# GDN inverse by levels: 64x64 array quarters replaced by block-diagonal operands in the full array

## The reference, cut to what matters

```python
def _gated_delta_rule(q, k, v, beta, g):
    q, k, v, beta, g = (_chunks(t.astype(F32)) for t in (q, k, v, beta, g))
    gc = jnp.cumsum(g, axis=-1)
    decay = jnp.exp(jnp.where(incl, gc[..., :, None] - gc[..., None, :], -jnp.inf))
    kb = k * beta[..., None]
    lhs = eye + jnp.einsum("nbhik,nbhjk->nbhij", kb, k) * decay * (1.0 - eye)
    solve = functools.partial(lax.linalg.triangular_solve, left_side=True, lower=True, unit_diagonal=True)
    u = solve(lhs, v * beta[..., None])
    w = solve(lhs, kb * jnp.exp(gc)[..., None])
    ...                                   # scan over the chunks with a state
def _gdn_mixer(...):
    qkv = jax.nn.silu(_dwconv(qkv, conv_w))
    q, k = _l2norm(q), _l2norm(k)         # x * rsqrt(sum x^2 + NORM_EPS)
    o = rule(q, k, v, ...) + reversed rule
    o = _rms(o) * norm_w * jax.nn.silu(z)
    return o @ w_out
```

## Time and profile before

| what | value |
|---|---|
| median of 3 runs | 1712.95 us (1711.44, 1712.95, 1870.54) |
| the profiled execution: its own time | 1710.5 us |
| its span, first to last instruction | 1708.7 us |
| mean granted TensorE clock | 0.989 of full speed |
| GDN loop, one turn | 86.7 us |

### The profile page before, as it was taken

One profiled execution on the slowest core, in us unless ns is written; L12 is line 12 of the kernel. 1 busy time (PEld: TensorE's weight loads), 2 busy tenths in 40 slices (PEclk: granted clock), 3 DMA queues, 4 the chain that ended last, 5 costly groups with the idle time before them and its releaser, 6 DMA issues.

```text
span 1708.7 us, 36355 instructions
## 1 busy us (share of the span) xinstructions
PE 1587.3 (93%) x14884; PEld 994.6 (58%) x14884; DVE 902.7 (53%) x1956; ACT 658.1 (39%) x1316; POOL 122.9 (7%) x315
## 2 busy tenths in 40 slices
PE   5999999999999999999999999999999889777798
PEld 2465555656545758676767676777744545343443
DVE  1373552826533758686868686868620642111173
ACT  2152532516213645555555555555510112111123
POOL 7000010000000000000000000000000012122100
PEclk9999999999999999999999999999999979999999
DMA  9340111202102211111111111111054579999941
GB/s 360 98 102 2 49 51 38 62 0 99 57 13 77 78 51 51 51 51 51 51 51 50 51 50 51 51 51 51 2 200 157 229 268 419 421 421 421 399 155 49
DMA packets 105461, 210.93 MB, mean 123 GB/s; under 512 B 10194, under 2 KB 78135, under 8 KB 92028
## 3 DMA queue, kind: packets, MB, share of 16 engines
q1 hardware_dynamic: 99256, 197.52, 31.9%
q0 software_dynamic: 4896, 8.40, 1.3%
q10 hardware_dynamic: 1188, 3.28, 0.5%
HBM read 203.80 MB, written 14.81 MB: 128 GB/s over the span
## 4 chain that ended last, share of the span: by engine, by line
PE 55%; DMA 10%; DVE 4%; ACT 1%; issue 1%; SPq 0%; DVEq 0%; POOL 0%; ACTq 0%; POOLq 0%
PE ps L1497 12%; DMA W<-in_moe_w_up_dram 10%; PE ps L1508 6%; PE ps L2536 5%; PE ps L1669 4%; PE ps L1638 4%; PE ps L3119 3%; PE ps L2933 3%; PE ps L506 2%; PE ps L1538 2%; PE ps L1519 1%; PE ps L1548 1%; PE ps L1560 1%; PE ps L1523 1%; PE ps L2946 1%
## 5 line engine op out<-in xcount | busy, mean ns | idle before, releaser
L1497 PE MATMUL ps<-hT,W 128*128 128x512 f32 x512 | 233.6, 601 | 2.2 <-ACTq L95 2.2
L1497 PEld LDWEIGHTS ps<-hT,W 128*128 128x128 f32 x512 | 96.2, 193 | 101.0 <-issue 99.2
L594 PE MATMUL ps<-hT,W 128*128 128x512 f32 x288 | 143.3, 612 | 0.0
L1508 PE MATMUL ps<-W,hT 128*128 128x256 f32 x512 | 123.7, 387 | 0.0
L2080 DVE SCALAR_TENSOR_TENSOR arena<-ps,arena 128x510 f32<-128x510 f32 (+1 forms) x128 | 95.4, 745 | 14.0 <-ACT arena L1799 10.6
L1508 PEld LDWEIGHTS ps<-W,hT 128*128 128x128 f32 x512 | 92.8, 190 | 12.7
L2536 PE MATMUL ps<-W,yT 128*128 128x512 f32 x216 | 93.1, 592 | 0.9 <-ACT yT L1892 0.9
L1902 ACT ACTIVATE W<-ps 128x512 f32<-128x512 f32 x96 | 57.5, 599 | 74.3 <-PE ps L1638 30.8
L1669 PE MATMUL ps<-W 64*64 64x64 f32 x2304 | 77.1, 220 | 0.0
L1638 PE MATMUL ps<-W,arena 64*64 64x64 f32 x2048 | 68.5, 220 | 6.6 <-DVE spare L189 2.5
L1669 PEld LDWEIGHTS ps<-W 64*64 64x64 f32 x2304 | 72.8, 135 | 2.7 <-issue 2.7
(11 more groups left out here) (543 smaller groups left out, 2896.0 us busy)
## 6 DMA issues: line engine op xcount, KB each, us to landing
W<-in_w_in_dram SPq DMA_DIRECT2D x33, 512.0 KB, 6.7
W<-in_gdn_w_in_dram SPq DMA_DIRECT2D x16, 1024.0 KB, 7.6
arena<-in_moe_w_up_dram SPq DMA_DIRECT2D x16, 1024.0 KB, 25.6
arena<-in_moe_w_down_dram SPq DMA_DIRECT2D x16, 1024.0 KB, 24.2
W<-in_moe_w_up_dram SPq DMA_DIRECT2D x16, 1024.0 KB, 25.3
W<-in_moe_w_down_dram SPq DMA_DIRECT2D x16, 1024.0 KB, 24.4
W<-in_moe_w_gate_dram SPq DMA_DIRECT2D x16, 1024.0 KB, 25.0
arena<-in_moe_w_gate_dram SPq DMA_DIRECT2D x14, 1024.0 KB, 25.5
```

Of the source, the lines that this page charges most:

```text
L594: mm = pe.matmul(ps[:, 5 + i % 2, :], w[:, k, j, :], hT[:, k, :], start=(k == 0), stop=(k == ND - 1))
L1497: mm = pe.matmul(ps[:, 6 + k0 % 2, :], wg[:, k, j * P:(j + 1) * P], hT[:, k, :], start=(k == 0), stop=(k == ND - 1))
L1508: mm = pe.matmul(ps[:, 4 if t < 2 else 1, 256 * (t % 2):256 * (t % 2) + 256], hT[:, k, t * P:(t + 1) * P], wz[:, k, :], start=(k == 0), st ...
```

## The change

For levels 1 to 4 both products use the whole array. `Nn` gets its two off-diagonal quarters cleared by POOL (`clear_corners`), after they were saved to a new tensor `corner` for level 6, so that one 128x128 by 128x64 product does both quarters of V. ACT writes V into a block-diagonal tensor `Vbd` (one copy for each half of the partitions), so that one product with V as the stationary operand does both quarters of T, and gives T itself instead of its transpose. DVE puts the new blocks into `Tgc` and transposes to `TTgc`; step `T g lv` now stands after the transpose. The two groups' V products come first, then z steps, then the two groups' T products; the z steps are dealt out anew, and `k_tokens` and `v_tokens` change places. The epsilons move into the bias of ACT's Ln, the norm weight into the scale of the copy to `yT`, so `norm_eps`, `z_weighted` and half of `o_mean` go. `first_level` of group 0 moves ahead of `output 3`, and the last convolution is split around level 1.

```diff
-    Vgc = half2[:, 4096:5120].rearrange("p (s m t) -> p s m t", s=2, m=8)
+    Vbd = [half2[:, 4096:5120].rearrange("p (m t) -> p m t", m=8), gate[:].rearrange("p (m t) -> p m t", m=8)]
...
-                pe.wait_ge(*s.dve.at("norm eps 0", s.i))
-                pe.wait_ge(*s.dve.at("norm eps 1", s.i))
+                pe.wait_ge(*s.act.at("norm ln 0", s.i))
+                pe.wait_ge(*s.act.at("norm ln 1", s.i))
...
-                        else:
-                            for m in range(8):
-                                for q in HALF:
-                                    mm = pe.matmul(small(3 * g, m)[q, :], Nn[q, 2 * g + m // 4, m % 4, q], TTgc[q, g, m, :], start=True, stop=True)
...
-                        if not top:
-                            pe.wait_ge(*s.dve.at(f"turned {g} {lv}", s.i))
...
-                            else:
-                                for q in (HALF[m % 4 // 2],) if top else HALF:
-                                    mm = pe.matmul(small(3 * g + 2, m)[q, :], Tgc[q, g, m, :], Vgc[q, g, m, :], start=True, stop=True)
...
+            zs = iter([(t, k) for t in (2, 3) for k in range(ND)])
+            def z_steps(n):
+                for t, k in (next(zs) for _ in range(n)):
+                    z_part(s, t, range(k, k + 1))
             for lv in range(1, LEVELS):
                 top, joined = lv == LEVELS - 1, lv == LEVELS - 2
+                for g in range(2):
+                    pe.wait_ge(*s.dve.at(f"T {g} {lv - 1}", s.i))
+                    if lv == 1:
+                        pe.wait_ge(*s.pool.at(f"corners {g}", s.i))
+                    if scan and lv == 1 and g == 0:
+                        pe.wait_ge(*s.act.at(f"v' {NT - 1}", s.i))
+                        pe.wait_ge(*s.dve.at(f"o {NT - 1}", s.i))
+                    pe.nop().then_inc(admitted, 1)
...
+                    else:
+                        for m in range(8):
+                            mm = pe.matmul(small(3 * g, m), Nn[:, 2 * g + m // 4, m % 4, :], TTgc[:, g, m, :], start=True, stop=True)
+                    mm.then_inc(*s.pe.step(f"V {g} {lv}"))
...
+                z_steps((2, 1, 2, 1, 2, 2)[lv - 1])
+                for g in range(2):
+                    pe.wait_ge(*s.act.at(f"T {g} {lv}" if top else f"V {g} {lv}", s.i))
+                    if scan and lv == 1 and g == 0:
+                        pe.wait_ge(*s.act.at(f"qS {NT - 1}", s.i))
+                    pe.nop().then_inc(admitted, 1)
+                    for m in (0, 2, 1, 3, 4, 6, 5, 7):
...
+                        else:
+                            mm = pe.matmul(small(3 * g + 2, m), Vbd[g][:, m, :], Tgc[:, g, m, :], start=True, stop=True)
+                    mm.then_inc(*s.pe.step(f"T {g} {lv}"))
                 if lv == 2:
+                    k_tokens(s)
+                if lv == 3:
                     v_tokens(s)
+                z_steps((3, 0, 1, 2, 0, 0)[lv - 1])
...
-            act.wait_ge(*s.dve.at(f"norm eps {j}", s.i))
-            link(act.activation(ctmp[j], ctmp[j], ACT.Ln), s.act)
+            act.wait_ge(*s.pe.at(f"norm {j}", s.i))
+            link(act.activation(ctmp[j], ps[:, 3 + PLACE[j], :], ACT.Ln, bias=neps[:, 0:1]), s.act, f"norm ln {j}")
...
-            act.activation(yT[:, k, :], ps[:, 3 + e, :], ACT.Copy).then_inc(*s.act.step(f"{kind}y {e}"))
+            act.activation(yT[:, k, :], ps[:, 3 + e, :], ACT.Copy, scale=nw[:, 0:1]).then_inc(*s.act.step(f"{kind}y {e}"))
...
-                    act.activation(Vgc[:, g, :, :].rearrange("p m t -> p (m t)"), ps[:, 3 * g, :], ACT.Copy).then_inc(*s.act.step(f"V {g} {lv}"))
+                    for q in HALF:
+                        act.activation(Vbd[g][q, :, q], ps[q, 3 * g, :].rearrange("p (m t) -> p m t", m=8), ACT.Copy).then_inc(*s.act.step(f"V {g} {lv}"))
...
-                    if g == 1 and lv == 1:
-                        sigmoid(s, 3)
-                    for k in {(2, 1): (0, 1), (3, 0): (2,), (3, 1): (3, 4), (4, 0): (5,), (4, 1): (6, 7)}.get((lv, g), ()):
-                        keep_v_tokens(s, k // 2, k % 2)
-                    if g == 0 and lv == 1 and scan:
-                        o_square(s)
-                    if g == 1 and lv == 3 and scan:
-                        o_rsqrt(s)
-                if lv == 3:
+                if lv == 1 and scan:
+                    o_square(s)
+                if lv == 2:
+                    sigmoid(s, 3)
                     act.wait_ge(*s.pe.at("k tokens", s.i))
                     act.activation(ktok.rearrange("p c t -> p (c t)"), ps[:, 4, :], ACT.Copy).then_inc(*s.act.step("k tokens"))
+                if lv in (4, 5):
+                    for k in range(4 * (lv - 4), 4 * (lv - 4) + 4):
+                        keep_v_tokens(s, k // 2, k % 2)
+                if lv == 4 and scan:
+                    o_rsqrt(s)
...
+        def clear_corners(s):
+            for g in range(2):
+                pool.wait_ge(*s.dve.at(f"N {2 * g}", s.i))
+                pool.wait_ge(*s.dve.at(f"N {2 * g + 1}", s.i))
+                for d, (to, of) in enumerate((HALF, HALF[::-1])):
+                    pool.tensor_copy(corner[of, g, :, :, :], Nn[of, 2 * g:2 * g + 2, 2 * d:2 * d + 2, to]).then_inc(*s.pool.step())
+                pool.wait_ge(*s.pool.last())
+                for to, of in (HALF, HALF[::-1]):
+                    pool.memset(Nn[of, 2 * g:2 * g + 2, :, to], 0.0).then_inc(*s.pool.step(f"corners {g}"))
...
-        def norm_eps(s, j):
-            dve.wait_ge(*s.pe.at(f"norm {j}", s.i))
-            dve.tensor_scalar(ctmp[j], ps[:, 3 + PLACE[j], :], NORM_EPS, None, ALU.add).then_inc(*s.dve.step(f"norm eps {j}"))
...
-        def z_weighted(s):
-            dve.wait_ge(*s.dve.at("silu z", s.i))
-            z8 = zg.rearrange("p c (e t) -> p (c e) t", e=2)
-            dve.tensor_tensor(z8, z8, repeat(nw, 8), ALU.mult).then_inc(*s.dve.step("z weighted"))
...
-            dve.copy_predicated(TTgc[:, g, :, :].rearrange("p (c b) t -> p c b t", c=2), masked(lv), tiles4(ps[:, 3 * g + 2, :]))\
-               .then_inc(*s.dve.step(f"T {g} {lv}"))
-            if lv < LEVELS - 2:
-                dve.wait_ge(*s.dve.at(f"T {g} {lv}", s.i))
-                dve.transpose(Tgc[:, g, :, :].rearrange("p m t -> p (m t)"), TTgc[:, g, :, :].rearrange("p m t -> p (m t)"))\
-                   .then_inc(*s.dve.step(f"turned {g} {lv + 1}"))
+            if lv == LEVELS - 2:
+                dve.copy_predicated(TTgc[:, g, :, :].rearrange("p (c b) t -> p c b t", c=2), masked(lv), tiles4(ps[:, 3 * g + 2, :]))\
+                   .then_inc(*s.dve.step(f"T {g} {lv}"))
+                return
+            dve.copy_predicated(Tgc[:, g, :, :].rearrange("p (c b) t -> p c b t", c=2), masked(lv), tiles4(ps[:, 3 * g + 2, :]))\
+               .then_inc(*s.dve.step(f"put {g} {lv}"))
+            dve.wait_ge(*s.dve.at(f"put {g} {lv}", s.i))
+            dve.transpose(TTgc[:, g, :, :].rearrange("p m t -> p (m t)"), Tgc[:, g, :, :].rearrange("p m t -> p (m t)")).then_inc(*s.dve.step(f"T {g} {lv}"))
...
-                for g in range(2):
-                    first_level(s, g)
+                first_level(s, 1)
             else:
                 masked_qk(s)
-            convolve(s, v1)
-            scan_columns(s, scan)
-            attention(s, 0, s)
+            convolve(s, v1, (1, 3))
...
+                if lv == 1:
+                    convolve(s, v1, (0, 4))
+                    scan_columns(s, scan)
                 if lv == 2:
+                    silu(s, v1)
+                    attention(s, 0, s)
+                if lv == 3:
                     attention(s, NT - 1, s)
-                if lv == 1:
-                    silu(s, v1)
-                if lv == 2 and scan:
-                    o_mean(s)
+                    if scan:
+                        o_mean(s)
...
+            first_level(s, 0)
```

More of the change, by code:

```diff
@@ L1341, in build @@
     pcg = take(QUANT, NT, 4)
-    nw = take(P)
+    nw = take(1)
     rsn = take(8)
@@ L1881, in o_rsqrt @@
         def o_rsqrt(s):
-            act.wait_ge(*s.dve.at("o eps", s.i))
-            link(act.activation(rsn, rsn, ACT.Ln), s.act)
+            act.wait_ge(*s.dve.at("o sums", s.i))
+            link(act.activation(rsn, rsn, ACT.Ln, scale=1.0 / P, bias=neps[:, 0:1]), s.act)
             act.activation(rsn, rsn, ACT.Exp, scale=-0.5).then_inc(*s.act.step("o rstd"))
@@ L2005, in _ @@
                 pool.wait_ge(*ab_pool.last())
+        for v in Vbd:
+            for q, o in (HALF, HALF[::-1]):
+                pool.memset(v[q, :, o], 0.0).then_inc(*ab_pool.step())
         ab_pool.close()
+        def clear_corners(s):
[7 more added lines that the diff above has]
+                    pool.memset(Nn[of, 2 * g:2 * g + 2, :, to], 0.0).then_inc(*s.pool.step(f"corners {g}"))
+        clear_corners(first)
+        first.pool.close()
+        pool.wait_ge(*first.pool.end())
+        loop.pool.credit(pool)
+        for i in range(LOOPS):
+            s = turn_of(i)
+            s.pool.begin(i)
+            clear_corners(s)
```

(12 more changed lines are left out.)

110 lines of the change are left out of this document (44 added, 66 removed).

## The result

| | before | after |
|---|---|---|
| median | 1712.2 us (4 runs, 1708.14 to 1870.54) | 1817.59 us (4 runs, 1812.51 to 1820.3) |
| span of the profiled run | 1708.7 us | 1815.6 us |
| one turn of the head loop | 86.73 us | 99.38 us |
| records of PE | 14884 | 12836 |

The changed kernel is slower: ratio 1.0617, 95% interval 1.0598 to 1.0636. The run of 1870.54 us was in a slower state and is left out of the ratio. A turn is measured from one head's transposes to `yT` to the next head's, over five turns (705.80 to 1139.45 before, 736.50 to 1233.41 after). It is 12.65 us longer, and seven turns are 88.6 of the 106.9 us by which the span grew.

A forecast was written before the change was run, and what follows sets the result against it. PE's work was taken to set the 86.70 us turn. 12.2 - 0.3 + 1.2 = 13.1 us a head, times 8 is +105 on 1710.5: 1815.5, with 2.45 to the median 1818 us; range 1794 to 1838.

The forecast's parts named there:

- The products: V and T of levels 1 to 4: full-array records take 110.4 ns, a stretch 1.767 us, +12.2 us a head.
- The covers: Levels 1 to 4: V copy, mask copy and transpose lie under PE work, only because the products have become slower.
- the gap ahead of `V 1 1` stays: Level 1, group 1: V still waits for the second first_level, which ends where it did.
- The start: Before level 1: first_level 0 ahead of output 3 starts PE about 0.3 us earlier; POOL's new work costs nothing.
- Levels 5 and 6: End of the levels: ACT's copies are late and four z steps become two; 10.4 us for 10.05, +1.2 a head.
- I count it like the others: First head: its own wait for DVE in level 1 comes only before V 1 1, so 13.1 us too.
- What is removed: First part of the turn: norm_eps and z_weighted leave DVE; at most 0.3 us a head, taken as 0.
- Moved columns set the pace: Rival for full-array products of levels 1 to 4: 54 ns a record, not slower, 1705 us; chance 0.04.

The follow-up runs named there:

- the four shapes: Changed kernel plus one overwritten stretch of 16 records, each in another shape, ahead of group 0's T products at each of levels 1 to 4: 1897.5 us.
- the two single runs: Changed kernel with only T, then only V, of levels 1 to 4 back to 64x64 quarters: 1776.8 us and 1780.9 us.
- the first experiment: Changed kernel with both products of levels 1 to 4 back to 64x64 quarters, the rest kept: 1740.51 us, 1.0168 of the kernel before.
- the run with the relief alone: Kernel before with only the epsilons in ACT's Ln bias and the norm weight in the copy to yT: 1713.17 us, ratio 1.0.

## Why the prediction was right, and where it was off

**The products.** The forecast took 110.4 ns for a record from the gate columns and got 1.767 us a stretch and +12.2 us a head. Measured: 110 ns, 1.76 us and +12.1. Taking the longest run of the same shape among the rows (97, 110.4, 112, 113) was right. The reason given, that the stationary columns set the pace, is shown by the four shapes, and the two single runs show that V and T carry it in nearly equal parts.

**The covers.** The forecast said that copy and transpose are covered only because the products have become slower. Two runs show it: levels 1 to 4 have 0.18 us of idle time in the changed kernel, and with short products the turn idles 1.2 us more. The expectation of the first experiment had up to 0.5 us a head and was short by more than the waits: 2.8 us a head came back in all. The wait for `first_level 1` at `V 1 1` (0.95 us in a turn there, 0.13 in the changed kernel) was not counted, nor were the 1.6 us of busy time. The forecast's sentence that the gap ahead of `V 1 1` stays is a misreading: in a loop turn of the kernel before there was none, since the three z steps filled it; in the changed kernel the slow `V 0 1` fills it.

**The start.** V starts 0.05 us after the last z product instead of 0.61, a gain of 0.56 us where 0.3 was said: the right mechanism, and a size nearly twice the one forecast. POOL was rightly costed at nothing; each copy takes 407 and each clear 519 ns, and group 0's are done at 976.8, 5.2 us ahead of V.

**Levels 5 and 6.** The term was +1.2 us a head, mostly for ACT's chain. Measured as the forecast counts it, the stretch is 10.24 us where 10.4 was laid out and 10.05 stood before, with two z steps (0.87 us) fewer inside, so the term is 1.1. The wait at the last T product is 1.03 us, where the layout had about 1.35. Moving v tokens gives back 0.53. The mechanism is right, but the idle time there rose by only 0.7 us, from 1.34 to 2.06, since PE's own pause in level 5 went away at the same time. The three terms, 12.1 - 0.56 + 1.1, make the 12.65 us of a turn, where 13.1 was said.

**The first head.** "I count it like the others" is the step that failed. It cost 18.05 us, not 13.1, and 4.7 of these come back when its wait is filled. The forecast named this wait, but not that it would grow to 2.86 us once its z steps had moved, nor that a lower clock would follow. The 4.95 us missed there cancelled in part against the 7 x 0.45 us over-counted in the turns. The forecast for the profiled execution, 1815.5 us, is 1.9 us below the 1817.4 measured. That the median, 1818 against 1817.59 us, is closer still is luck: the forecast adds 2.45 us from execution to median, and here it was 0.2.

**What is removed.** Costed at 0 a head; the run with the relief alone says 1.0 within 0.16%.

**The rivals.** Moved columns set the pace: refuted by the shapes, 106 to 111 ns for 32, 64 and 128 columns. The rule of the Trainium skill, "TensorE: Matmul & The Clock Gate", section "The mechanism", that loads overlap running products only in another row group, does not hold here: at 1.76 us a stretch, full-array loads of 192 ns follow each other every 110 ns. The same page's section "LDWEIGHTS (loading the stationary operand)" says that the time of a load in ns goes by its columns over 1.2 and not by its rows, by which, as an estimate, 128 columns take 107 ns and 64 take 53. The pace of the shapes agrees roughly: 106 to 121 ns for 128 columns, 67 for 64. The recorded length of a load does not: 192 ns for 128x128, 138 for 128 rows x 64 columns.

## What to carry to other kernels

In these fp32 runs, a product that moves 128 columns or fewer is paid by its stationary columns. Merging two 64x64 quarters into one block-diagonal 128x128 product halved the instructions and cost 75% more time: two alternating quarters take 63 ns as a pair, one full record 110. A record with 64 stationary columns and all rows takes 67 ns. If fewer rows save nothing here either, one quarter alone would take as long, and a pair at 63 ns must overlap. That the quarters overlap because they lie in different rows and columns is likely, but not shown: no run puts quarters one after another in the same place. Before merging, look in the trace for any line of the new shape, however far away in the program, and take the pace from start to start of a long run of it. And when a slower engine hides a longer chain, test the rest of the change with the old products, or its cost is found only when someone makes them fast again.

## What the runs showed of the hardware

The granted clock fell where PE had no idle time. In the run of the shapes, in the fifth and sixth turn, it fell after the added 32-column products and again after the added products of 64 rows, although the records stood back to back; in the seventh it fell after the latter only. The turn grew from 106.3 to 112.9 us (timeline of PE in the fifth turn, then windows):

```profile
1130.26 1.98 PE L1682 MATMUL ps<-W 128*128 128x64 f32 x16
1132.07 3.43 PE L1682 MATMUL ps<-W,gate 128*128 128x64 f32 x16
1135.29 2.87 PE L1509 MATMUL ps<-W,hT 128*128 128x256 f32 x6
```

```profile
1129.00:1135.00 6.00, 6.00 (x44) 6.00 (x44) 1.50 (x3) 1.10 (x2) 0.00 (x0) 0.77 0.01 3
1135.00:1140.00 5.00, 5.00 (x23) 4.46 (x23) 3.41 (x7) 0.00 (x0) 0.00 (x0) 0.59 0.00 0
```

Before it fell, PE had run stretches of full-array products that moved 64 and 32 columns each. The changed kernel itself, without the added stretches, kept 1.00 in its loop turns from 635 us on. Why the clock fell here is open: the same four shapes ran at 1.00 in the first four turns. The pace that the stationary columns set follows the clock: at 0.50 the same 16 records took 3.64 us instead of 1.76.

Idle time came before a lower clock in three places: 2.86 us in the first head, and 2.2 and 2.3 us at the start of the first loop turn in the two kernels. After 1.18 us of idle time, in the first head of the kernel before, it stayed at 1.00.

An activation of 64 partitions took as long as one of 128 (593 against 599 ns for 512 columns), so splitting a copy by partitions doubled it.
